# Full-precision products for the context keys in the first attention of a two-block transformer kernel

## The reference, cut to what matters

```python
def latent_attention(q, k_all, v_all):      # q: 1024 queries; k_all, v_all: 1024 + 256 keys
    ...
    scale = HEAD_QK ** -0.5                  # HEAD_QK = 96
    def one_block(qblk):                     # 128 queries
        s = jnp.einsum('bqhd,bkhd->bhqk', qblk, k_all, preferred_element_type=jnp.float32) * scale
        p = jax.nn.softmax(s, axis=-1).astype(v_all.dtype)
        return jnp.einsum('bhqk,bkhd->bqhd', p, v_all)
```

## Time and profile before

| | |
|---|---|
| median of three executions | 3566.63 us |
| profiled execution, its own time | 3566.49 us |
| its span | 3564.7 us |
| PE busy | 3135.7 us (88%) |
| DVE busy | 1641.6 us (46%) |
| ACT busy | 908.4 us (25%) |
| POOL busy | 1075.9 us (30%) |
| `values`, line 976 | 640 products, 85.8 us |
| transposes, line 964 | 640 products, 83.4 us |
| low parts of `Ea`, 512 and 256 columns | 128 and 64 subtractions |

### The profile page before, as it was taken

How to read it: one execution, slowest core, us unless ns; L and a number is a source line. 1 busy time by engine, 2 the same in 40 slices (tenths; PEclk the granted TensorE clock), 3 DMA queues, 4 the chain that set the end, 5 groups by cost and what they waited for, 6 DMA issues and landing times.

```text
span 3564.7 us, 38200 instructions
## 1 busy us (share of the span) xinstructions
PE 3135.7 (88%) x14989; PEld 2586.6 (73%) x14989; DVE 1641.6 (46%) x2274; ACT 908.4 (25%) x1462; POOL 1075.9 (30%) x482
## 2 busy tenths in 40 slices
PE   3579999899988799999999899978899999989795
PEld 2467877688877588888887677657688777767583
DVE  7786220288854531313132343453435666553434
ACT  1031221166620310101011101210334545542202
POOL 4523226500022243444443333124231121212141
PEclk7699999899999899999999999989899999999897
DMA  4434344523123011111111111101141212111011
GB/s 179 160 112 162 104 167 141 140 63 86 40 83 124 30 48 51 50 47 47 47 52 43 48 42 54 42 24 48 35 149 54 54 54 56 52 42 42 18 47 71
DMA packets 114051, 258.80 MB, mean 73 GB/s; under 512 B 46817, under 2 KB 64817, under 8 KB 110081
## 3 DMA queue, kind: packets, MB, share of 16 engines
q1 hardware_dynamic: 113664, 256.95, 23.1%
q10 hardware_dynamic: 256, 0.07, 0.0%
HBM read 214.54 MB, written 42.38 MB: 72 GB/s over the span
## 4 chain that ended last, share of the span: by engine, by line
PE 75%; DVE 15%; ACT 4%; issue 3%; POOL 1%; DMA 1%; DVEq 0%; SPq 0%; ACTq 0%; POOLq 0%
PE ps L324 22%; PE ps L326 21%; PE ps L325 21%; ACT tmp L1328 2%; DVE tmp L1917 2%; PE ps L976 2%; PE ps L1238 2%; DVE Ea L1725 2%; DVE tmp L2204 1%; PE ps L1224 1%; PE ps L964 1%; PE ps L1116 1%; DVE rs L1322 1%; DVE acc L1728 1%; DVE accx L1753 1%
## 5 line engine op out<-in xcount | busy, mean ns | idle before, releaser
L660 POOL TENSOR_TENSOR whi<-raw,onesf 128x1024 fp32r<-128x1024 f32 x235 | 451.1, 1920 | 2396.0 <-PE ps L326 2300.5
L662 POOL TENSOR_TENSOR wlo<-raw,whi 128x1024 fp32r<-128x1024 f32 x235 | 612.6, 2607 | 18.4
L324 PE MATMUL ps<-Hb_hi,whi 128*128 128x512 f32 x1424 | 571.2, 401 | 32.9 <-DVE Hb_lo L1297 17.6
L326 PE MATMUL ps<-Hb_hi,wlo 128*128 128x512 f32 x1424 | 557.6, 392 | 0.0
L325 PE MATMUL ps<-Hb_lo,whi 128*128 128x512 f32 x1424 | 557.4, 391 | 0.0
L324 PEld LDWEIGHTS ps<-Hb_hi,whi 128*128 128x128 f32 x1424 | 269.4, 189 | 91.1 <-issue 27.5
L326 PEld LDWEIGHTS ps<-Hb_hi,wlo 128*128 128x128 f32 x1424 | 268.9, 189 | 57.7
L325 PEld LDWEIGHTS ps<-Hb_lo,whi 128*128 128x128 f32 x1424 | 269.6, 189 | 50.3
L1328 ACT ACTIVATE tmp<-ps 64x256 f32<-64x256 f32 (+1 forms) x120 | 81.6, 680 | 642.3 <-PE ps L326 572.6
L1328 ACT ACTIVATE tmp<-tmp,mx 128x1280 f32<-128x1280 f32 (+2 forms) x192 | 187.1, 975 | 108.3 <-DVE mx L2204 90.0
L324 PE MATMUL ps<-Uhi,whi 128*128 128x512 f32 x512 | 199.2, 389 | 0.0
(11 more groups left out here) (388 smaller groups left out, 6208.8 us busy)
## 6 DMA issues: line engine op xcount, KB each, us to landing
raw<-in_w SPq DMA_DIRECT2D x221, 512.0 KB, 3.6
adas<-in_ada SPq DMA_DIRECT2D x24, 1024.0 KB, 5.0
raw<-in_w SPq DMA_DIRECT2D x36, 256.0 KB, 4.0
gate_d<-gst SPq DMA_DIRECT2D x16, 512.0 KB, 3.0
v_d<-VS SPq DMA_DIRECT2D x2, 4096.0 KB, 14.9
ncB<-cum_d SPq DMA_DIRECT2D x16, 512.0 KB, 3.7
Vx<-v_d SPq DMA_DIRECT2D x16, 512.0 KB, 4.6
kn_d<-stg SPq DMA_DIRECT2D x10, 512.0 KB, 5.3
```

What stands on the lines that cost most here:

```text
L324: nc.tensor.matmul(o, wh, xh, start=start, stop=False)
L326: return nc.tensor.matmul(o, wl, xh, start=False, stop=stop)
L660: nc.gpsimd.tensor_tensor(whi[b][:, 0:w], raw[b][:, 0:w], onesf[:, 0:1].to_broadcast([P, w]), ALU.mult).then_inc(S("split_hi"), 1)
L662: nc.gpsimd.tensor_tensor(wlo[b][:, 0:w], raw[b][:, 0:w], f32(whi[b][:, 0:w]), ALU.subtract).then_inc(S("split"), 1)
```

## The change

In the first attention the turned exponentials of the two context key tiles are no longer split. ACT copies the third group of transposes from PSUM into a new tile `Ec` in plain 32-bit type; DVE makes no low part for that group; `values` multiplies it with `Va`, both read as plain 32-bit, in one product a key tile instead of two reduced ones. `Ec` lies where the last two key tiles of `Ea`'s low part lay. The counts of `ml_lo` go from three to two a slot, and where the third subtraction was waited for, ACT's third copy now is.

```diff
+        Ec = [at(f"Ec{j}", 64 + 20 * j + 18, [P, 2, CTX]) for j in range(2)]
 def flips(t):
     pe.wait_ge(S("ml_e"), t + 1)
     for g in range(3):
-        if t:
-            pe.wait_ge(S("ml_lo"), 3 * (t - 1) + g + 1)
+        if t and g < 2:
+            pe.wait_ge(S("ml_lo"), 2 * (t - 1) + g + 1)
+        elif t:
+            pe.wait_ge(S("ml_hi"), 3 * t)
 def values(u):
-    pe.wait_ge(S("ml_lo"), 3 * (2 * u + 2))
+    pe.wait_ge(S("ml_lo"), 2 * (2 * u + 2))
+    pe.wait_ge(S("ml_hi"), 3 * (2 * u + 2))
     pe.wait_ge(S("ml_x"), 2 * min(2 * u + 3, SLOTS - 1) + 1)
     o = ps[:, 4 * HALF + CTX:5 * HALF]
-    for kt in range(10):
+    for kt in range(8):
         for n in range(2):
-            last = nc.tensor.matmul(o, Va[h % 2][:, kt, :], Ea[u % 2][n][:, kt, :], start=kt == 0 and n == 0, stop=kt == 9 and n == 1)
+            nc.tensor.matmul(o, Va[h % 2][:, kt, :], Ea[u % 2][n][:, kt, :], start=kt == 0 and n == 0, stop=False)
+    for kt in range(8, 10):
+        last = nc.tensor.matmul(o, f32(Va[h % 2][:, kt, :]), Ec[u % 2][:, kt - 8, :], start=False, stop=kt == 9)
 def flip_hi(t):        # ACT
-        copy(Ea[u % 2][0][:, k[0]:k[-1] + 1, P * (t % 2):P * (t % 2) + P],
+        copy(Ea[u % 2][0][:, k[0]:k[-1] + 1, P * (t % 2):P * (t % 2) + P] if g < 2 else Ec[u % 2][:, :, P * (t % 2):P * (t % 2) + P],
 def flip_lo(t):        # DVE
-    for g in range(3):
+    for g in range(2):
```

## The result

The changed kernel takes 3570.9 us in the median of 20 runs (3565.76 to 3575.15), the kernel before 3560.7 us in 20 runs beside them (3555.25 to 3569.84). The ratio is 1.0027, 95% interval 1.002 to 1.0034: 7 to 12 us slower, 9.6 us in the middle. The forecast was +9.4 us.

A forecast was written before the change was run, and what follows sets the result against it. The prediction took a loop of waits in the first attention, with the exponential binding, as the bound. Block +12.8 us less 3.4 given back makes +9.4, 3576 us (+0.26%); forecast's own range 3573 to 3580, overall range 3565 to 3588.

The forecast's parts named there:

- What binds: First attention, plain pairs of 9.10 us: the exponential, not DVE's subtraction, releases the transposes; the block counts in full.
- the two ends: Plain pair: exponential's accumulator read ends at 852.44, subtractions at 852.48 us; the first transpose needs only the first subtraction.
- The block: Block of values on PE: four full-precision instructions add 0.88, four removed products save 0.48; +0.40 us, 12.8 over 32.
- the bounds of 0.12 and 0.43: Limits in us for one 256-column full-precision instruction: replaced instruction's price, and the 512-column price if nothing scales; 0.22 taken.
- Given back: DVE's late places: 2.6 us in 7 multiplication pairs, 0.4 behind conversions, 0.35 at the end; 3.4 us together.
- The small stall of 0.13: Pair after a conversion pair, 9.23 us: PE's stall on DVE's addition goes, 0.4 us in all.
- the idle time stays: Three conversion pairs of 11.22 us: values' 1.39 us idle stays, since the subtraction ended before ACT's conversion.
- After the stage the rest of the kernel shifts as a whole: After the first attention: PE continues with products not needing it, so the rest only shifts, with no DMA newly late.
- A: Subtraction binds the even tile's transposes: 0.35 us a pair returns, 3565 us, chance 0.08; odd tiles too, 3554, 0.02.
- B: Full-precision instructions in the block do not scale or their loads are not hidden: 15 us more, 3591 us, chance 0.12.
- D: The new products are issued single-pass, two fewer per block: -7.7 us, with the give-back 3555 us; chance 0.02.
- C: Nothing given back (3.4 us), or two more clock dips at idle places (2.8 us): 3579 us; chance 0.16.

The follow-up runs named there:

- products alone: Changed kernel's full-precision products, with DVE's third subtraction and PE's wait for it kept; against the kernel before: 3570.89 against 3561.24 us, ratio 1.0023.
- relief alone: Kernel before without DVE's third subtraction, still 20 single-pass products, context low products reading the high part again; 3558.2 against 3561.24 us, ratio 0.999.
- one more subtraction: Kernel before with a fourth 256-column DVE subtraction a tile, written aside ahead of the third; 3563.05 against 3560.88 us, ratio 1.0007.
- the six runs without the move: Against before: full-precision products only 1.0023; third subtraction removed 0.999; 18 products 0.9972; six full-precision key tiles 1.0079; fourth subtraction 1.0007; changed kernel, fewer waits 1.0022.

## Why the prediction was right

- **What binds.** That the exponential and not the subtraction releases the transposes, against the chain view, held: products alone 1.0023, relief alone 0.999, one more subtraction 1.0007, plain pairs 9.48, 9.10 and 9.10 us. The 0.04 us between the two ends was the whole question; the order of the waits gave the answer, and the runs bear it out. They show that the subtraction does not bind a plain pair. That the exponential does is read from its end, just ahead of the first weight load, and from the releaser that PE names; no run made it shorter or longer.
- **The block.** Forecast +0.40 us, measured +0.375: 0.217 us an instruction instead of 0.22. 32 blocks make 12.0 instead of 12.8 us. Half the price of the 512-column product was the right scale; the bounds of 0.12 and 0.43 were both far off. The estimate by the warm gap of the Trainium skill ("TensorE: Matmul & The Clock Gate", Back-to-back issue gap), which the section gives for a product by itself, was 0.216 an instruction when taken for two passes over 256 columns, and the trace agrees with 0.217; for the reduced 256-column product it has 0.109 where the trace has 0.12, and the sum went by the trace.
- **Given back.** The sum was right, its places only partly. The four pairs with DVE's product alone are 9.48 us, so their 0.37 is gone. The three with a conversion came to 11.11; I had them at about 11.25 (11.22 + 0.40 - 0.37). The pair after them has no stall beyond the clock's. The last block follows after 5.53 us against 5.50, so it got 0.35 back. Against a block that is 0.375 longer, that is 4 x 0.37 + 3 x 0.48 + 3 x 0.13 + 0.35 = 3.7 us, where 3.4 were forecast.
- **But not for the reason given.** With the subtraction kept, the pairs with DVE's product still are 9.49 us. In the changed kernel the later scores remove that stall by themselves, and the relief adds only 0.1 us at each conversion and 0.33 at the end. In the kernel before, the relief alone removes it too (9.09 us). The prediction named both causes together; the two runs show that either is enough. The small stall of 0.13 behind a conversion goes by the later scores only: 9.46 us with the products alone, but still 9.24 with the relief alone. That "the idle time stays" at a conversion was right (1.39 us in all these runs), but the relief alone shortens that pair by 0.48 us where 0.37 were counted.
- **Missed.** "After the stage the rest of the kernel shifts as a whole" was wrong by 0.9 us: PE's program is 8 instructions longer, the MLP's loop loads instructions in every round, and it takes 599.3 instead of 598.4 us. With 32 to 40 instructions more than before it took 7 to 16 us more.
- **The sum.** 12.0 - 3.7 + 0.9 = 9.2 us, and 9.6 measured (7 to 12). That the forecast of 9.4 came so close is in part luck: the block was put 0.8 too high, the give-back 0.3 too low, and the MLP's 0.9 was not in it. The absolute forecast of 3576 us is 5 above the measured 3570.9, because the three executions that it started from had a median of 3566.6 where 20 have 3560.7. Its own range of 3573 to 3580, which misses the measured time, was also wider than its terms: 0.39 to 0.46 for the block give 3576 to 3578. Rivals A, B and D are out. The clock's dips (C) are real, 1.3 to 1.5 us each in these two kernels, but the profiles have none to three of them with the same idle time ahead, and they carry no systematic part of the result that these runs can show.

## What to carry to other kernels

Where the chain of waits names a releaser whose end lies within a few hundredths of a microsecond of another's, read the order of the waits in the code: it tells whether taking work from that engine pays. A full-precision product of 256 columns costs 0.43 us against 0.24 for the two reduced ones that it replaces, so it is free only where PE has cover. Here it had none; with eight products of the block moved ahead of the transposes it had (8.73 us a pair with either kind of product). Moving that part of the block into PE's idle microsecond, with the half copy moved too and the surplus waits left out, was worth 18 us. Compare stages that the edit does not touch as well, and the packets of the instruction queue: here 32 more instructions ahead of a loop took back almost half of a gain of 18 us.

## What the runs showed of the hardware that was not expected

- PE's idle time at the turns of an untouched loop changed with the number of instructions in PE's program: 598.4 us at 22249 and 22369 instructions, 599.3 to 599.5 at 22377, 605.0 and 606.8 at 22401, 613.1 and 614.2 at 22409. The instruction queue moved 86 or 87 packets in the first case and 114 in all others; the 27 more fall inside the loop, where the first case has none from 1380 to 1900 us (the kernel before).
- Idle time of 1.39 us on PE, the same three places in each of eight kernels (before, changed, and the six runs without the move), was followed by half the full clock for 3.4 us at 10 of the 24 places, none to three in a profile, and left it alone at the others. A dip cost 1.2 to 1.6 us.
